# A fused two-layer block on one core: order of VectorE's compressed weights, TensorE's last modulation columns, and the first two half tiles of a mixer

## The chip, the cores and the metric

The kernel runs as one program on one core of a Trainium2 chip. The metric is the device time of one execution in microseconds. The kernel before took 1382.02 us, the median of three runs (1380.93 to 1382.14). All numbers of the profile come from one execution of their own, which took 1381.31 us.

## The reference, cut to what matters

Two different transformer blocks are run one after the other on x of 512 tokens and 1024 features, in float32.

```
x -> first block:  h = rms_norm(x); proj = h @ w_in
       attention over compressed, selected and window keys, each with a gate:
         kc, vc = compress(k_cmp), compress(v_cmp)          # 31 compressed positions
         p_c = softmax(q . kc - slope * distance) * valid   # "compressed weights"
         o = g0 * (p_c @ vc) + g1 * o_selected + g2 * o_window
       a causal convolution branch, a gated merge, w_out, residual
       conv FFN: w_up (1024 x 5632), 3 taps, silu(a) * v, w_down (2816 x 1024), residual
       final rms_norm
  -> second block: mod = silu(c) @ ada_w + ada_b             # 6 x 1024 "modulation"
       h = rms_norm(x) * (1 + scale) + shift
       proj = h @ w_in_2                                     # first tiles: the f logits
       sliding window attention, HGRN recurrence, w_out_2, gate, residual
       conv FFN with modulation, final rms_norm
```

With 8 blocks of 64 keys and a choice of 16, all blocks are selected, so the selected branch is causal attention over all keys, and so is the window branch.

## The kernel before, in words

Each weight matrix is cut into tiles of 128 output columns, numbered s through the whole program (`S_MERGE`, `S_DOWN`, `S_FH` and so on are first numbers of stages). A tile holds up to eight k of 128 rows. Every product is split for precision: ScalarE copies a raw tile to `w_hi` (L855), GpSimd subtracts to get `w_lo` (L788, function `lo`), and TensorE does three matmuls per k, `split_product` (L2135 to L2137): `w_hi` with `h_hi`, `w_hi` with `h_lo`, `w_lo` with `h_hi`. Each engine runs its own list in order; they meet at semaphores. ScalarE writes `w_hi` four tiles ahead, and `lo` follows it.

**Attention items.** The 32 items of the first block are (pair of heads, tile of queries, branch). In item j TensorE does the scores of j into banks 4 and 5 (two groups; it must wait until VectorE's row minimum of item j - 1 has read that bank), then half a merge tile (four k), then turns the weights of item j - 1 (L2408), which needs their scaling by VectorE, and in every second item multiplies two items with the values (L2379). The first four items have branch 0; from item 4 on, turns of the compressed weights `cp` (L2402) come in, and they need the semaphore `cp_ready` at 2. ScalarE does the exponentials (L1022), a copy (L1060) and in odd items a `w_hi`. VectorE's loop (from L1645) has in item j: `row_minimum(j)` (L1540), in items 1 to 4 one part of `compressed_weights` (two groups, each with a first part L1624 to L1630 and a second part L1620), convolution taps (L1527, from item 4), the copy of the turned weights of j - 1 (L1670) and `scaled_weights(j)` (L1636, L1640).

**Down projection of the first block.** 24 down parts of seven or eight k each; the modulation of the second block is computed beside them. SyncE loads 128 columns of `ada_w_2`, VectorE multiplies and adds them over eight k (`ada_reduce`, L1746 to L1756, into `ada_sum`), TensorE sums over partitions (`ada_tile`, L2440, one column of bank 6). The order of both is written out: TensorE takes column `m` after part n by the loop at L2522, VectorE by the same kind of loop. When all 48 are done VectorE forms shift and gain (L1850 to L1854).

**Into the next mixer.** The last down parts and the first four tiles of the second block (`S_FH`) are done in halves of 256 tokens, so that norm and matmul overlap. VectorE and ScalarE make 16 pieces of h (8 k for each half of the tokens): L1376, L900, L1386. TensorE's half tiles of half 0 wait for one piece per k. `column_sums(1)` (L2511) sums the squares of the second half and waits for `sums_added` (L1833, L1834); mean, root and inverse follow, then the turned inverses (L2519), then the pieces of half 1. For half 1, `second_halves` already takes the first two tiles in turn: k 0 to 3 of one, k 0 to 3 of the other, then k 4 to 7 alternating.

Of the kernel before, what the change touches and what calls it, by code (L numbers as in the profile page):

```python
# [18 lines left out]
KD = D // P  # L19
QT = T // P  # L20
# [23 lines left out]
S_FH, S_QH, S_KV2, S_PAIRED, S_GH = 126, 130, 134, 136, 144  # L44
# [114 lines left out]
def build(nc, a, out):  # L159
# [5 lines left out]
    with ctx:  # L165
# [24 lines left out]
        h_hi = sb("h_hi", [P, KD, T], F32R)  # L190
        msk_f = sb("msk_f", [P, DH], at=offset[0])
        yT = sb("yT", [P, KD, T], at=offset[0])
        h_lo = sb("h_lo", [P, KD, T], F32R)
# [1156 lines left out]
        def _(dve):  # L1350
# [261 lines left out]
            def compressed_weights(g, part):  # L1612

                x = cp[:, g * 16:(g + 1) * 16, 0:NCMP]
                low = stat[:, 32 + 16 * g:48 + 16 * g]
                if part:
                    for t in range(QT):
                        xt = cp[:, g * 16 + t * 4:g * 16 + t * 4 + 4, 0:NCMP]
                        v = cvalid[:, t, 0:NCMP].unsqueeze(1).to_broadcast([P, 4, NCMP])
                        ins = dve.tensor_tensor(xt, xt, v, ALU.mult)  # L1620
                    ins.then_inc(cp_ready, 1)
                    return
                dve.wait_ge(cexp_done, g + 1)
                link(dve.tensor_reduce(low, x, AX.X, ALU.add))  # L1624
                link(dve.reciprocal(low, low))
                dve.wait_ge(sig_ready, 1)
                gc = gates[:, :, 12 * g:12 * g + 12].rearrange("p t (i c) -> p t i c", c=3)[:, :, :, 0]
                by_tile = low.rearrange("p (t i) -> p t i", t=QT)
                link(dve.tensor_tensor(by_tile, by_tile, gc, ALU.mult))
                link(dve.tensor_tensor(x, x, low.unsqueeze(2).to_broadcast([P, 16, NCMP]), ALU.mult))  # L1630

            def scaled_weights(j):
                i, t, b = ITEMS1[j]
                q = 2 * (j % 2)
                dve.wait_ge(exp_done, 2 * j + 2)
                link(dve.reciprocal(stat[:, 8 + q:10 + q], stat[:, 4 + q:6 + q]))  # L1636
                for g in range(2):
                    x = sc[:, j % 2, g, 0:(t + 1) * P]
                    n = 12 * g + 3 * i + 1 + b
                    ins = dve.tensor_scalar(x, x, stat[:, 8 + q + g:9 + q + g], gates[:, t, n:n + 1], ALU.mult, ALU.mult)  # L1640
                ins.then_inc(p_ready, 1)
# [3 lines left out]
            for j in range(1, NI + 1):  # L1645
                if j < NI:
                    row_minimum(j)
                if j < 5:
                    compressed_weights((j - 1) // 2, (j - 1) % 2)
                if 4 <= j and IN_PSUM[1] + j - 4 < CONV_W:  # L1650
                    taps(1, IN_PSUM[1] + j - 4, IN_PSUM[1] + j - 3)
                c = j - LN_ADD + 1
                if 1 <= c < CC:
                    dve.wait_ge(tap_done, CC * CONV_W)
                    if c > 1:
                        dve.wait_ge(acc_added, c - 1)
                    dve.tensor_tensor(rstd[:, :], acc[:, 0, :] if c == 1 else rstd[:, :], acc[:, c, :],
                                      ALU.add).then_inc(acc_added, 1)
                c = j - LN_SQUARE - 1
                if 1 <= c < CC:  # L1660
                    dve.wait_ge(ln_sq, c + 1)
                    if c > 1:
                        dve.wait_ge(acc_added, CC + c - 2)
                    dve.tensor_tensor(z[:, 0, 0:T], z[:, 0, 0:T], z[:, c, 0:T], ALU.add).then_inc(acc_added, 1)
                m = j - 1
                L2 = (ITEMS1[m][1] + 1) * P
                dve.wait_ge(pw_turned, m + 1)
                if m >= 2:
                    dve.wait_ge(pv_done, m - 1)
                dve.tensor_copy(pT[:, m % 2, 1, 0:L2], ps[7][:, 0:L2]).then_inc(pw_copied, 1)  # L1670
                if j < NI:
                    scaled_weights(j)
                if j in LN_MEAN:
                    half = LN_MEAN.index(j)
                    cols = slice(half * 256, half * 256 + 256)
                    dve.wait_ge(ln_sum, half + 1)
                    for c in range(CC):
                        dve.scalar_tensor_tensor(out=acc[:, c, cols], in0=ps[3][:, cols], scalar=-1.0 / CONV_CH,
                                                 in1=acc[:, c, cols], op0=ALU.mult, op1=ALU.add).then_inc(ln_centred, 1)
                if j == LN_SUM:  # L1680
                    dve.wait_ge(ln_sqsum, 1)
                    dve.tensor_copy(stat[:, LN_SUMS], ps[3][:, 0:QT]).then_inc(ln_centred, 1)
# [449 lines left out]
        def _(pe):  # L2132
# [39 lines left out]
                elif s < s0 + KD and b != 1:  # L2172
                    ins.then_inc(half_done, 1)

            def second_halves(s, x, xl, ready):

                cols = COLS[1]
                for k, n in [(k, 0) for k in range(4)] + [(k, 1) for k in range(4)] + [(k, n) for k in range(4, KD) for n in range(2)]:
                    if n == 0:
                        ready(k)  # L2180
                    ins = split_product(ps[BANK[s + n]][:, cols], w_hi[(s + n) % 4][:, k, :], w_lo[(s + n) % 4][:, k, :],
                                        x[:, k, cols], xl[:, k, cols], k == 0, k == KD - 1)
                    if k == KD - 1:
                        ins.then_inc(tile_done, 1)

            def first_sum(b):
# [263 lines left out]
            def ffn_pe(s0, b):  # L2450
                for half in range(2):
                    for j in range(4):
                        if (half, j) == (1, 0):
                            second_halves(s0, h_hi, h_lo, lambda k: pe.wait_ge(half_lo, PIECES * b + KD + k + 1))
                        if half and j < 2:
                            continue
                        half_tile(b, s0 + j, half, h_hi, h_lo,
                                  ready=(lambda k: pe.wait_ge(half_lo, PIECES * b + KD * half + k + 1)) if j == 0 else None)
                        if (half, j) == (0, 1):
                            second_sum(b)  # L2460
                        if (half, j) == (1, 3) and b == 0:
                            ada_tile(ADA_EARLY - 1, (ADA_EARLY - 1) % 2, ADA_EARLY)
                with pe.Fori(0, FT // 2 - 1) as i:
                    for j in range(4):
                        s = s0 + 4 + j
                        pe.wait_ge(lo_done, i * 4 + (s + 1))
                        pe.wait_ge(freed["dve"], i * 4 + (FREED[s][1] - 4))
                        for k in range(KD):
                            ins = split_product(ps[BANK[s]][:, :], w_hi[s % 4][:, k, :], w_lo[s % 4][:, k, :],
                                                h_hi[:, k, :], h_lo[:, k, :], k == 0, k == KD - 1)  # L2470
                        ins.then_inc(tile_done, 1)
                        if b == 0 and j % 2:
                            n = ADA_EARLY + j // 2
                            ada_tile(i * 2 + n, n % 2, i * 2 + (n + 1))
# [47 lines left out]
            next_ada = itertools.count(ADA_EARLY + ADA_UP - 2)  # L2522
            for n in range(20):
                down_part(S_DOWN, n, parts(g_lo_done, 2) if n in (0, 2, 4) else None)
                if n < 18:
                    for _ in range(2 if n and n % 4 == 0 else 1):
                        m = next(next_ada)
                        ada_tile(m, m % 2, m + 1)
            for n in range(20, 24):
# [3 lines left out]
                if n == 20:  # L2533
                    column_sums(0)
            for half in range(2):
                for j in range(4):
                    if (half, j) == (1, 0):
                        second_halves(S_FH, h_hi, h_lo, lambda k: pe.wait_ge(half_lo, PIECES + KD + k + 1))
                    if half and j < 2:
                        continue  # L2540
                    half_tile(1, S_FH + j, half, h_hi, h_lo,
                              ready=(lambda k: pe.wait_ge(half_lo, PIECES + KD * half + k + 1)) if j == 0 else None,
                              between=(lambda: turn_inverse(1, 7, 2, range(2, QT))) if (half, j) == (0, 2) else None)
                    if (half, j) == (0, 1):
                        column_sums(1)
                    if (half, j) == (0, 3):
                        turn_inverse(1, 6, 0, range(QT))
            for s in range(S_QH, S_KV2):
                tile(s, h_hi, h_lo)

# [229 lines left out]
```

## Time and profile before

| what | before |
|---|---|
| median of the runs | 1382.02 us |
| profiled execution | 1381.31 us |
| its span | 1379.3 us |
| TensorE matmuls busy | 1367.5 us (99%) |
| VectorE busy | 770.4 us (56%) |
| ScalarE busy | 599.2 us (43%) |
| GpSimd busy | 600.4 us (44%) |
| granted TensorE clock | 9 tenths or more in all 40 slices |

The span runs from the first to the last instruction; the rest of the execution's time lies around it. Busy time of TensorE counts modelled ends of pipelined matmuls, so neighbouring ones overlap. In a timeline, a row is one instruction or several of a kind in sequence, with start, duration, engine and line; in brackets stands the idle time of the engine before it and what ended it. L numbers are lines of the kernel before.

### The profile page before, as it was taken

How to read it: one execution, taken by the hardware profiler on the slowest of the kernel's cores; microseconds unless marked ns; L12 is line 12 of the kernel's file. 1: busy time of each engine (PE TensorE's matmuls, PEld its weight loads, DVE VectorE, ACT ScalarE, POOL GpSimd, SP SyncE). 2: the span in 40 equal slices, each digit the busy share in tenths (PEclk: the TensorE clock that was granted, in tenths of full speed). 3: DMA queues.
4: the chain of work that ended last, by engine and by line, in shares of the span. 5: the costliest groups of instructions: out<-in, count | busy, mean ns of one | idle time of the engine just before them, and what ended most of it. 6: DMA issues, size and time to landing. Idle time of an engine off the chain costs nothing.

```text
span 1379.3 us, 20888 instructions
## 1 busy us (share of the span) xinstructions
PE 1367.5 (99%) x7650; PEld 1142.9 (83%) x7650; DVE 770.4 (56%) x1524; ACT 599.2 (43%) x1030; POOL 600.4 (44%) x322
## 2 busy tenths in 40 slices
PE   8999999999999999999999999999999999999998
PEld 7877777778998888888889978878998888888887
DVE  5897965456677566666873868633563223231222
ACT  6223555464254445443222524575364434442222
POOL 7532222226254444444543479623354444444441
PEclk9999999999999999999999999999999999999999
DMA  6931011015525444445662141021223332222221
GB/s 214 228 93 62 31 62 46 25 38 168 168 94 166 139 147 150 146 129 170 196 203 92 62 122 62 32 62 31 92 78 106 106 107 91 91 87 96 99 84 62
DMA packets 188309, 146.15 MB, mean 106 GB/s; under 512 B 21561, under 2 KB 186659, under 8 KB 188240
## 3 DMA queue, kind: packets, MB, share of 16 engines
q1 hardware_dynamic: 186528, 144.59, 34.0%
q8 instruction: 47, 0.77, 0.2%
q10 hardware_dynamic: 1200, 0.36, 0.1%
q0 software_dynamic: 512, 0.25, 0.1%
q14 instruction: 22, 0.18, 0.0%
HBM read 143.08 MB, written 2.10 MB: 105 GB/s over the span
## 4 chain that ended last, share of the span: by engine, by line
PE 91%; DVE 5%; DMA 3%; issue 1%; ACT 0%; DVEq 0%; ACTq 0%
PE ps L2135 27%; PE ps L2137 26%; PE ps L2136 26%; DMA ada<-in_ada_w 3%; DVE ps L1751 2%; PE ps L2584 2%; PE ps L2324 2%; PE ps L2379 1%; PE ps L2408 1%; PE ps L2655 1%; PE ps L2611 1%; PE ps L2640 1%; PE ps L2677 0%; PE ps L2218 0%; PE ps L2570 0%
## 5 line engine op out<-in xcount | busy, mean ns | idle before, releaser
L788 POOL TENSOR_TENSOR w_lo<-raw,w_hi 128x1024 fp32r<-128x1024 f32 (+2 forms) x224 | 515.4, 2304 | 709.0 <-ACT w_hi L855 439.4
L2135 PE MATMUL ps<-h_hi,w_hi 128*128 128x512 f32 (+1 forms) x1336 | 504.0, 377 | 0.6 <-DVE h_lo L1386 0.6
L2136 PE MATMUL ps<-h_lo,w_hi 128*128 128x512 f32 (+1 forms) x1336 | 493.4, 369 | 0.0
L2137 PE MATMUL ps<-h_hi,w_lo 128*128 128x512 f32 (+1 forms) x1336 | 493.2, 369 | 0.0
L2135 PEld LDWEIGHTS ps<-h_hi,w_hi 128*128 128x128 f32 x1336 | 251.7, 188 | 60.8 <-issue 17.6
L2137 PEld LDWEIGHTS ps<-h_hi,w_lo 128*128 128x128 f32 x1336 | 251.8, 188 | 43.1
L2136 PEld LDWEIGHTS ps<-h_lo,w_hi 128*128 128x128 f32 x1336 | 251.9, 189 | 40.1 <-issue 0.5
L855 ACT ACTIVATE w_hi<-raw 128x1024 fp32r<-128x1024 f32 (+2 forms) x136 | 133.7, 985 | 254.5 <-PE ps L2137 245.1
L1125 ACT ACTIVATE w_hi<-raw 128x1024 fp32r<-128x1024 f32 x88 | 93.2, 1059 | 217.9 <-PE ps L2137 217.9
L2135 PE MATMUL ps<-g_hi,w_hi 128*128 128x512 f32 (+1 forms) x394 | 146.6, 372 | 0.0
L2136 PE MATMUL ps<-g_lo,w_hi 128*128 128x512 f32 (+1 forms) x394 | 144.6, 367 | 0.0
L2137 PE MATMUL ps<-g_hi,w_lo 128*128 128x512 f32 (+1 forms) x394 | 144.4, 367 | 0.0
L1751 DVE SCALAR_TENSOR_TENSOR ps<-ada,cond,ps 128x128 f32<-128x128 f32 x288 | 102.5, 356 | 10.3
L2137 PEld LDWEIGHTS ps<-g_hi,w_lo 128*128 128x128 f32 x394 | 74.3, 188 | 12.2
L2135 PEld LDWEIGHTS ps<-g_hi,w_hi 128*128 128x128 f32 x394 | 74.3, 189 | 11.7
L2136 PEld LDWEIGHTS ps<-g_lo,w_hi 128*128 128x128 f32 x394 | 74.4, 189 | 11.5
L1790 DVE SCALAR_TENSOR_TENSOR sq<-ps,small,sq 128x511 f32<-128x511 f32 x44 | 33.0, 750 | 88.4 <-ACT sq L1132 85.4
L2060 DVE SCALAR_TENSOR_TENSOR xT<-ps,small,xT 128x256 f32<-128x256 f32 (+1 forms) x22 | 13.3, 604 | 106.1 <-PE ps L2137 106.1
L1527 DVE SCALAR_TENSOR_TENSOR ps<-z,small,ps 128x512 f32<-128x512 f32 x106 | 70.4, 747 | 0.0
L1784 DVE TENSOR_TENSOR hn<-ps,sq 128x512 f32<-128x512 f32 x22 | 15.2, 691 | 85.9 <-ACT sq L1136 85.9
L1022 ACT ACTIVATE sc<-sc,stat 128x128 f32<-128x128 f32 (+3 forms) x64 | 35.5, 555 | 35.0 <-DVE stat L1540 34.9
L1670 DVE COPY pT<-ps 128x128 f32<-128x128 f32 (+3 forms) x32 | 15.7, 490 | 54.3 <-PE ps L2379 32.1
(362 smaller groups left out, 1700.8 us busy)
## 6 DMA issues: line engine op xcount, KB each, us to landing
ada<-in_ada_w SPq DMA_DIRECT2D x48, 512.0 KB, 3.8
raw<-in_ffn_w_up SPq DMA_DIRECT2D x22, 1024.0 KB, 4.9
raw<-in_w_up SPq DMA_DIRECT2D x22, 1024.0 KB, 4.9
raw<-in_w_in SPq DMA_DIRECT2D x21, 1024.0 KB, 5.0
raw<-in_ffn_w_down SPq DMA_DIRECT2D x8, 896.0 KB, 6.2
raw<-in_w_down SPq DMA_DIRECT2D x8, 896.0 KB, 4.7
raw<-in_w_in SPq DMA_DIRECT2D x16, 256.0 KB, 3.8
raw<-in_w_out SPq DMA_DIRECT2D x4, 1024.0 KB, 5.2
```

What stands on the lines that cost most here:

```text
L788: pool.tensor_tensor(w_lo[slot % 4][:, 0:nk, :], part[:, :, slot % 2 * P:(slot % 2 + 1) * P], w_hi[slot % 4][:, 0:nk, :].bitcast(F32), ALU ...
L855: act.activation(w_hi[s % 4][:, 0:nk, :], part[:, :, s % 2 * P:(s % 2 + 1) * P], ACT.Copy).then_inc(hi_done, 1)
L1022: act.activation(x, x, ACT.Exp, scale=-1.0, bias=stat[:, 2 * (j % 2) + g:2 * (j % 2) + g + 1], accum_out=stat[:, 4 + 2 * (j % 2) + g:5 + 2 ...
L1125: act.activation(w_hi[s % 4][:, :, :], part[:, :, s % 2 * P:(s % 2 + 1) * P], ACT.Copy).then_inc(hi_done, 1)
L1527: ins = dve.scalar_tensor_tensor(out=out, in0=src, scalar=w, in1=was, op0=ALU.mult, op1=ALU.add)
L1751: dve.scalar_tensor_tensor(out=acc, in0=src, scalar=c, in1=acc, op0=ALU.mult, op1=ALU.add).then_inc(ada_scaled, 1)
L1790: dve.scalar_tensor_tensor(out=u[:, t, 1:T], in0=src[:, 0:T - 1], scalar=col(wname, m + wide), in1=u[:, t, 1:T], op0=ALU.mult, op1=ALU.add ...
L2135: pe.matmul(out_ap, w, x, start=first, stop=False, **kw)
L2136: pe.matmul(out_ap, w, xl, start=False, stop=False, **kw)
L2137: return pe.matmul(out_ap, wl, x, start=False, stop=last, **kw)
L2324: pe.matmul(ps[4 + g][:, 0:L], qT[grp, i, t * P:(t + 1) * P], kT[grp, b, 0:L], start=True, stop=True).then_inc(qk_done, 1)
L2584: ins = pe.matmul(bank[:, at:at + nq], keys[:, hd, t * P:(t + 1) * P], qd[n % 2][:, hd, q0:q0 + nq], start=True, stop=True)
```

## The change

Three orders are changed; no instruction is added or removed.

1. VectorE, items 1 to 4: the part of `compressed_weights` moves from behind the row minimum of item j to behind the scaling of item j.
2. TensorE, down parts: columns are taken two at a time after parts 4, 8 and 12 only, and one after parts 16, 17 and 18 each, in place of two after 16 and one after 17.
3. TensorE, first half of the tokens in the next mixer: tiles `S_FH` and `S_FH + 1` are taken in turn (`second_halves` becomes `two_halves`, used for both halves).

```diff
-                if j < 5:
-                    compressed_weights((j - 1) // 2, (j - 1) % 2)
                 if 4 <= j and IN_PSUM[1] + j - 4 < CONV_W:
                     taps(1, IN_PSUM[1] + j - 4, IN_PSUM[1] + j - 3)
...
                 if j < NI:
                     scaled_weights(j)
+                if j < 5:
+                    compressed_weights((j - 1) // 2, (j - 1) % 2)
...
-            def second_halves(s, x, xl, ready):
-
-                cols = COLS[1]
+            def two_halves(s, half, x, xl, ready):
+
+                cols = COLS[half]
                 for k, n in [(k, 0) for k in range(4)] + [(k, 1) for k in range(4)] + [(k, n) for k in range(4, KD) for n in range(2)]:
                     if n == 0:
                         ready(k)
+                    if half == 0 and k == 0:
+                        pe.wait_ge(lo_done, s + n + 1)
+                        wait_bank(pe, s + n)
                     ins = split_product(ps[BANK[s + n]][:, cols], w_hi[(s + n) % 4][:, k, :], w_lo[(s + n) % 4][:, k, :],
                                         x[:, k, cols], xl[:, k, cols], k == 0, k == KD - 1)
-                    if k == KD - 1:
+                    if k == KD - 1 and half:
                         ins.then_inc(tile_done, 1)
...
-                if n < 18:
-                    for _ in range(2 if n and n % 4 == 0 else 1):
+                if n < 19:
+                    for _ in range(2 if n in (4, 8, 12) else 1):
                         m = next(next_ada)
                         ada_tile(m, m % 2, m + 1)
...
             for half in range(2):
-                for j in range(4):
-                    if (half, j) == (1, 0):
-                        second_halves(S_FH, h_hi, h_lo, lambda k: pe.wait_ge(half_lo, PIECES + KD + k + 1))
-                    if half and j < 2:
-                        continue
+                two_halves(S_FH, half, h_hi, h_lo, lambda k: pe.wait_ge(half_lo, PIECES + KD * half + k + 1))
+                if half == 0:
+                    column_sums(1)
+                for j in range(2, 4):
                     half_tile(1, S_FH + j, half, h_hi, h_lo,
-                              ready=(lambda k: pe.wait_ge(half_lo, PIECES + KD * half + k + 1)) if j == 0 else None,
                               between=(lambda: turn_inverse(1, 7, 2, range(2, QT))) if (half, j) == (0, 2) else None)
-                    if (half, j) == (0, 1):
-                        column_sums(1)
-                    if (half, j) == (0, 3):
-                        turn_inverse(1, 6, 0, range(QT))
+                if half == 0:
+                    turn_inverse(1, 6, 0, range(QT))
```

The call in the up projections' `ffn_pe` becomes `two_halves(s0, 1, ...)` with the same order as before.

## Rows read from the trace of the kernel before

**Rows 1.** Page: busy us (share of span) x instructions.
```profile
PE 1367.5 (99%) x7650; PEld 1142.9 (83%) x7650; DVE 770.4 (56%) x1524; ACT 599.2 (43%) x1030; POOL 600.4 (44%) x322
```

**Rows 2.** Waits of TensorE: waited for: us in total, times, longest.
```profile
PE ps L2440 <- DVE ada_sum L1756: 1.0, 1, 1.0
```

**Rows 3.** Timeline of TensorE, items 3 to 5: start us, us, what [idle].
```profile
141.55 1.13 PE L2324 MATMUL ps<-kT,qT 64*128 64x512 f32 x4
...
147.06 0.49 PE L2324 MATMUL ps<-kT,qT 64*128 64x128 f32 x4
...
150.11 0.39 PE L2137 MATMUL ps<-h_hi,w_lo 128*128 128x512 f32 x1
151.44 1.09 PE L2408 MATMUL ps<-ident,sc 128*128 128x128 f32 x8 [0.94 <-DVE sc L1640]
152.46 0.70 PE L2324 MATMUL ps<-kT,qT 64*128 64x256 f32 x4
...
155.97 0.38 PE L2402 MATMUL ps<-ident,cp 128*31 128x128 f32 x2
```

**Rows 4.** Timeline of VectorE, items 2 and 3.
```profile
139.82 0.55 DVE L1540 CUSTOM_DVE_ANT_0 sc<-ps,sq 128x384 f32<-128x384 f32 x1
...
140.77 2.47 DVE L1620 TENSOR_TENSOR cp<-cp,cvalid 128x124 f32<-128x124 f32 x4
...
145.69 0.66 DVE L1624 TENSOR_REDUCE stat<-cp 128x16 f32<-128x496 f32 x1
...
146.68 0.18 DVE L1629 TENSOR_TENSOR stat<-stat,gates 128x16 f32<-128x16 f32 x1
146.89 0.67 DVE L1630 TENSOR_TENSOR cp<-cp,stat 128x496 f32<-128x496 f32 x1
...
148.26 3.12 DVE L1640 TENSOR_SCALAR sc<-sc,stat,gates 128x512 f32<-128x512 f32 x2
```

**Rows 5.** Timeline of GpSimd, the same stretch.
```profile
140.12 2.38 POOL L788 TENSOR_TENSOR w_lo<-raw,w_hi 128x1024 fp32r<-128x1024 f32 x1 [7.67 <-ACT w_hi L855]
148.26 2.39 POOL L788 TENSOR_TENSOR w_lo<-raw,w_hi 128x1024 fp32r<-128x1024 f32 x1 [5.75 <-ACT w_hi L855]
```

**Rows 6.** Timeline of ScalarE: ends of the exponentials of items 2 and 3.
```profile
141.53 0.19 ACT L1022 ACTIVATION_READ_ACCUMULATOR sc<-sc,stat 128x1 f32 x1
...
146.53 0.19 ACT L1022 ACTIVATION_READ_ACCUMULATOR sc<-sc,stat 128x1 f32 x1
```

**Rows 7.** Timeline of TensorE, modulation columns behind down parts 15 and 16.
```profile
718.30 0.28 PE L2440 MATMUL ps<-ones,ada_sum 128*128 128x1 f32 x2
718.44 0.48 PE L2135 MATMUL ps<-g_hi,w_hi 128*128 128x512 f32 x1
...
723.31 0.28 PE L2440 MATMUL ps<-ones,ada_sum 128*128 128x1 f32 x2
...
724.79 0.49 PE L2135 MATMUL ps<-g_hi,w_hi 128*128 128x512 f32 x1
```

**Rows 8.** Timeline of TensorE, first two half tiles of the next mixer.
```profile
762.06 0.28 PE L2135 MATMUL ps<-h_hi,w_hi 128*128 128x256 f32 x1
...
762.42 0.28 PE L2135 MATMUL ps<-h_hi,w_hi 128*128 128x256 f32 x1
...
765.50 0.39 PE L2135 MATMUL ps<-h_hi,w_hi 128*128 128x256 f32 x1 [0.29 <-DVE h_lo L1386]
...
769.46 0.50 PE L2511 MATMUL ps<-ones,rstd 128*128 128x1 f32 x4
```

**Rows 9.** Timeline of VectorE, last piece and last square sum.
```profile
765.60 0.48 DVE L1386 SCALAR_TENSOR_TENSOR h_lo<-ps,small,h_hi 128x256 fp32r<-128x256 f32 x1 [0.15 <-ACT h_hi L900]
...
767.59 0.48 DVE L1834 SCALAR_TENSOR_TENSOR sq<-hn,stat,sq 128x256 f32<-128x256 f32 x1
```

**Rows 10.** Timeline of GpSimd, `w_lo` of the second and fourth tile.
```profile
758.42 2.41 POOL L788 TENSOR_TENSOR w_lo<-raw,w_hi 128x1024 fp32r<-128x1024 f32 x1 [1.21 <-ACT w_hi L855]
...
767.90 2.42 POOL L788 TENSOR_TENSOR w_lo<-raw,w_hi 128x1024 fp32r<-128x1024 f32 x1 [4.21 <-ACT w_hi L855]
```

More of the change, by code:

```diff
@@ L2453, in ffn_pe @@
                         if (half, j) == (1, 0):
-                            second_halves(s0, h_hi, h_lo, lambda k: pe.wait_ge(half_lo, PIECES * b + KD + k + 1))
+                            two_halves(s0, 1, h_hi, h_lo, lambda k: pe.wait_ge(half_lo, PIECES * b + KD + k + 1))
                         if half and j < 2:
```

## The prediction

> **What bounds the kernel now.** I read the page's busy shares first: TensorE (PE) is busy for 1367.5 us of a span of 1379.3 us [rows 1]. So nothing is won by making another engine faster; only places where TensorE stands still can move the end. The second view is the list of who waited for whom, cut to TensorE. The change touches three entries of it: 1.0 us for `ada_sum` [rows 2], 0.9 us for `sc`, which the timeline prints as idle time [rows 3], and short waits for `h_lo`, one of which stands in [rows 8]. The third view is the timeline around each of them, one engine at a time, because a wait that is removed has to be followed to whatever is late next. TensorE's modelled ends hide part of a wait (the idle time printed is measured from a modelled end), so I measure a wait as actual start minus the start that the regular spacing would give. The reader should check in the timelines that matmuls of 512 columns start every 0.23 us and those of 256 columns every 0.12 us (0.36 us for the three products of one k) [rows 3, 8].
>
> **Edit 1: compressed weights behind the scaling (items 1 to 4).** VectorE's order in item j was: row minimum of j, compressed weights, copy of the turned weights, scaling of j. The wait it is about: the turns of item 3 start at 151.44, where the last product before them started at 150.11, so they were due at 150.34 and are 1.10 us late; they wait for the scaling of item 3, which took 3.12 us for two products [rows 3, 4]. That scaling is long not because of work put before it but because GpSimd's `w_lo` ran from 148.26 to 150.65 [rows 5]. The same is seen at 140.77, where four products of `cp` and `cvalid` took 2.47 us while GpSimd's `w_lo` lasted from 140.12 to 142.50 [rows 4, 5]. So an instruction of VectorE with two inputs in SBUF that starts inside a `w_lo` finishes only after it. The reductions and the row minimum (one input in PSUM) are not held: the row minimum at 139.82 has its usual 0.55 us [rows 4].
>
> Now the new order. In item 1 the scaling ends at about 139.82, where the row minimum of item 2 used to start [rows 4]. The compressed weights of group 0 stand there now. By their rows in item 3, the first small product (`stat`, `gates`) starts 0.99 us after the reduction and the large one ends 1.87 us after it [rows 4]. So the small product would start at 140.81, inside the `w_lo` that ScalarE's work, which the edit does not touch, starts at 140.12 [rows 5]. It is held to 142.54, and the large one then needs 0.67 us: 143.25. Only then comes the row minimum of item 2; its first group needs 0.55 us and is done at 143.83. TensorE needs exactly this before the scores of item 3 may overwrite their bank, and these scores were issued at 141.55 [rows 3]. They go at 143.89: **+2.34 us**. Queued behind them in TensorE's order is a quarter of the merge tiles, the turns and the value products, all of which shift.
>
> From there: the exponentials of item 2 end 1.35 us after its first row minimum (141.72 [rows 6] against 140.37), so they end at 145.2; the scaling of 2, the second part of the weights (unheld some 0.8 us: 2.47 us less the 1.73 us up to 142.50) and the row minimum of 3 follow and end at 148.3; TensorE reaches the scores of item 4 at 147.06 + 2.34 = 149.40 [rows 3] and does not wait. The exponentials of 3 end at 149.24 (146.72 before [rows 6]), the scaling of 3 at 150.6. GpSimd's `w_lo` follows them by way of ScalarE's copy and `w_hi`, so it slips by the same 2.52 us to 150.78: it misses the scaling. TensorE wants it at 150.34 + 2.34 = 152.68, so the old wait goes: **-1.10 us**. What is late next: compressed weights of group 1 start at 150.47, their small product at 151.46 falls into the slipped `w_lo` (to 153.17), they end at 153.92, the row minimum of item 4 at 154.23; the scores of item 5 would be due at 152.46 + 1.24 = 153.70 [rows 3] and go at 154.29: **+0.59 us**. Last, the second part for group 1 now ends after taps, copy and scaling of item 4, at 157.93, against 155.97 + 1.83 = 157.80 for the turns that read it [rows 3]: **+0.13 us**. Sum for edit 1: **+1.96 us**. I find no later wait that absorbs it, since TensorE has none in the rest of this stage [rows 2].
>
> Bounds. If nothing of the compressed weights were held by `w_lo`, the weights would end at 139.82 + 1.87 = 141.69, the row minimum of 2 would be ready at 142.29 and the scores late by 0.80 us, the 1.10 us would go, and no other wait would form: -0.30 us. If the slipped `w_lo` also caught the scaling of item 3 (it would have to start before 150.06, not at 150.78), the weights of group 1 would end 0.6 us later: +2.6 us. I take +1.96, nearest to the rows, which show the hold with every start known.
>
> One operation has no held example in these rows: the small product of 16 elements. If only the large one were held, all would be 0.2 us earlier.
> The Trainium skill, page "SBUF — State Buffer", section "Who interferes with whom", says that a VectorE instruction with two SBUF inputs contends with a GpSimd instruction that reads SBUF, that whoever starts first keeps the pair of ports for its whole length, and it names no least size. By that rule the small product is held too (the 2.34 us as above; 2.1 us without it). It is the rule that speaks against this edit, and rows 4 and 5 agree with it in the two long groups.
>
> **Edit 2: last modulation columns.** After down part 16 TensorE did two columns (45 and 46), after part 17 one (47). The first started at 723.31; an unhindered column costs 0.14 us on TensorE (718.30 to 718.44); the tile behind the second started at 724.79. So 724.79 - 723.31 - 0.27 = **-1.21 us** goes when column 46 is taken after part 17 [rows 7]. VectorE finished column 46 just before 724.6, and part 17 now ends near 728.5. Column 47 met no wait at its old place behind part 17 (it is no entry of [rows 2]) and is now taken a whole part later. So no wait replaces this one. VectorE then folds the 48 columns into the modulation, which the first half pieces need only at 756. Bounds: 1.0 us (the printed idle [rows 2]) to 1.21 us.
>
> **Edit 3: first two half tiles of the next mixer in turn.** Before, TensorE went through eight k of the first half tile alone, from 762.06, at the pace at which VectorE and ScalarE deliver pieces of h, then through the second half tile, and reached the column sums at 769.46 [rows 8]. Unhindered, 16 k of 0.36 us end at 762.06 + 5.76 = 767.82: 1.64 us of waiting. In the new order k 0 to 3 of both tiles come first, so piece 4 is wanted at 764.94, 5 at 765.66, 6 at 766.38 and 7 at 767.10; the last piece is done at 766.08 [rows 9]. None is late. The second tile's `w_lo` is done at 760.83 [rows 10], before 763.50, when TensorE turns to that tile. But the column sums behind them need VectorE's last square added, which ends at 767.59 + 0.48 = 768.07 whatever TensorE does [rows 9]. TensorE goes on at 768.12: **-1.34 us**, and 0.3 us turn into a new wait. From the sums on, every step (means, root, inverse, pieces of the second half) is started by TensorE and moves with it. Bounds: -1.64 us to the rival below. Instructions are only reordered: none is added in edit 1, 2 or 3.
>
> **Sum.** +1.96 - 1.21 - 1.34 = -0.59 us. The profiled execution took 1381.31 us (span 1379.3 us and 2.0 us around it), so it would become 1380.7 us. It lies 0.7 us under the median 1382.02 of the runs shown; from the median the forecast is **1381.4 us**, which is no change: 0.2% (2.8 us) is about what can be told apart.
>
> **Rivals.**
> A. The hold does not strike the compressed weights, and edit 1 is a small gain: -0.30 - 1.21 - 1.34 = -2.85, so 1379.2 us. For it: the small product was never seen held. Against it: the four `cvalid` products right beside it were.
> B. Slower: a `w_lo` catches the last square sum. Today the product at 767.59 starts 0.3 us before GpSimd's `w_lo` at 767.90 (2.42 us) [rows 9, 10]. If that order turned, the sum would end at 770.6 instead of 768.07, TensorE would reach the column sums 1.1 us later than before instead of 1.34 earlier: +1.96 - 1.21 + 1.1 = +1.9, 1383.9 us. It decides as soon as `w_lo` starts before 767.59. Against it: both hang on the same square of ScalarE, and neither is moved by TensorE.
> C. The turn-taking gains nothing, since the wait for pieces merely moves to the column sums: +1.96 - 1.21 = +0.75, 1382.8 us. Against it: the square sum is ready 1.4 us before TensorE used to come.
> D. Edit 1 does what its order suggests, the wait of 1.10 us goes and no row minimum is late: -1.10 - 1.21 - 1.34 = -3.65, 1378.4 us. Against it: the compressed weights stand between two row minima in either order, and 1.9 us of them now delay the one that TensorE needs first.
>
> **How the numbers follow.** Forecast 0.68, A 0.10, D 0.05, B 0.08, C 0.09. Faster by over 0.2% needs A or D: 0.13, with A on the line. Slower by over 0.2% (past 1384.8) needs B with edit 1 at its upper bound: 0.05. Within: 0.82. The range runs from near A to B: 1378.9 to 1384.0.
>
> **What would show it.** Right: a TensorE wait of about 2.3 us before scores of item 3, released by VectorE's row minimum; `stat` or `cp` products of the compressed weights about 1.8 us long beside `w_lo`; no wait before the turns of item 3; no wait over 0.2 us at the last modulation columns; no `h_lo` wait in the first half tiles and a wait of about 0.3 us at the column sums. Wrong: the scores of item 3 start near 141.6 or 142.3, or the column sums near or after the 769.5 of before (less what came earlier).

## The result, and the profile after

| | before | after |
|---|---|---|
| median of 12 runs each, same chips | 1380.95 us (1379.62 to 1384.11) | 1383.58 us (1383.39 to 1385.32) |
| profiled execution, span | 1381.31, 1379.3 us | 1383.87, 1381.8 us |
| TensorE busy | 1367.5 us | 1370.3 us |
| mean granted clock of TensorE in it | 1.000 | 0.997 |

The ratio is 1.0018 [1.0009, 1.0026]: slower by 2.5 us, where no change (-0.6 us) was forecast. A repeat (below) gave 1.0017 [1.0008, 1.0026]. No instruction was added, yet TensorE, which is nearly always busy, is busy for 2.8 us more. So part of the loss is slower work and not standing still.

The busy line of the profile's page after, then TensorE's waits (waited for: total, times, longest):

```profile
PE 1370.3 (99%) x7650; PEld 1144.8 (83%) x7650; DVE 772.1 (56%) x1524; ACT 598.9 (43%) x1030; POOL 601.7 (44%) x322
```
```profile
PE ps L2327 <- DVE stat L1540: 2.7, 2, 2.3
```

The waits for `ada_sum` [rows 2] and `h_lo` of the half tiles [rows 8] are gone, and one for the row minimum is there, twice. TensorE's timeline around both (L2327 is L2324 of before, L2411 is L2408; answers to [rows 3]):

```profile
140.49 0.60 PE L2411 MATMUL ps<-ident,sc 128*128 128x128 f32 x4
143.34 2.08 PE L2327 MATMUL ps<-kT,qT 64*128 64x512 f32 x4 [2.25 <-DVE stat L1540]
145.36 0.79 PE L2135 MATMUL ps<-h_hi,w_hi 128*128 128x512 f32 x1
145.95 0.63 PE L2136 MATMUL ps<-h_lo,w_hi 128*128 128x512 f32 x1
146.38 0.63 PE L2137 MATMUL ps<-h_hi,w_lo 128*128 128x512 f32 x1
...
147.93 0.39 PE L2135 MATMUL ps<-h_hi,w_hi 128*128 128x512 f32 x1
...
153.90 0.39 PE L2137 MATMUL ps<-h_hi,w_lo 128*128 128x512 f32 x1
154.13 1.04 PE L2411 MATMUL ps<-ident,sc 128*128 128x128 f32 x8
155.66 0.91 PE L2327 MATMUL ps<-kT,qT 64*128 64x256 f32 x4 [0.49 <-DVE stat L1540]
```

Two things are to be seen. The turns of item 3 now follow their neighbour by 0.23 us: their old wait is gone. And the products of 512 columns start 0.43 us apart from 145.95 to 147.66, then 0.23 us again. The granted clock shows it too (a row is window: its length, then busy us and instructions of PE, PEld, DVE, ACT and POOL, then PEclk, the DMA share and GB/s):

```profile
143.00:148.00 5.00, 4.66 (x11) 2.70 (x12) 4.15 (x16) 2.89 (x9) 0.00 (x0) 0.66 0.00 0
148.00:153.00 5.00, 5.00 (x37) 3.95 (x36) 2.33 (x6) 2.12 (x4) 0.96 (x1) 1.00 0.01 3
```

The records put TensorE at half clock (1.2 GHz) from 144.33 to 147.74, and at the full 2.4 GHz on both sides. The execution of before has no such stretch between its first 10 us and its last two.

VectorE, and GpSimd beside it, show where the wait comes from (answers to [rows 4, 5]):

```profile
139.28 0.66 DVE L1624 TENSOR_REDUCE stat<-cp 128x16 f32<-128x496 f32 x1
139.98 0.25 DVE L1625 RECIPROCAL stat<-stat 128x16 f32<-128x16 f32 x1
140.26 1.72 DVE L1629 TENSOR_TENSOR stat<-stat,gates 128x16 f32<-128x16 f32 x1
142.01 0.67 DVE L1630 TENSOR_TENSOR cp<-cp,stat 128x496 f32<-128x496 f32 x1
142.72 0.56 DVE L1540 CUSTOM_DVE_ANT_0 sc<-ps,sq 128x384 f32<-128x384 f32 x1
...
143.21 0.55 DVE L1540 CUSTOM_DVE_ANT_0 sc<-ps,sq 128x384 f32<-128x384 f32 x1
...
152.18 0.66 DVE L1624 TENSOR_REDUCE stat<-cp 128x16 f32<-128x496 f32 x1
...
153.16 1.39 DVE L1629 TENSOR_TENSOR stat<-stat,gates 128x16 f32<-128x16 f32 x1
```
```profile
139.58 2.36 POOL L788 TENSOR_TENSOR w_lo<-raw,w_hi 128x1024 fp32r<-128x1024 f32 x1 [7.66 <-ACT w_hi L855]
152.04 2.48 POOL L788 TENSOR_TENSOR w_lo<-raw,w_hi 128x1024 fp32r<-128x1024 f32 x1 [10.10 <-ACT w_hi L855]
```

The product of 16 elements, 0.18 us long when free [rows 4], takes 1.72 and 1.39 us and ends with the `w_lo` beside it. The reduction at 152.18 starts inside the same `w_lo` and takes the 0.66 us that it takes elsewhere. The row minimum that the prediction gives for this, at 139.82, began before the `w_lo` of 140.12 and could not tell; one that begins inside a `w_lo`, at 155.35 in e7 below, takes 0.42 us, as its like at 155.49 in the kernel before, which had none beside it.

The other two edits. TensorE at the modulation columns behind parts 15 and 16 (answers to [rows 7]), then at the end of the first two half tiles ([rows 8]):

```profile
721.66 0.28 PE L2443 MATMUL ps<-ones,ada_sum 128*128 128x1 f32 x2
721.80 0.48 PE L2135 MATMUL ps<-g_hi,w_hi 128*128 128x512 f32 x1
...
726.67 0.28 PE L2443 MATMUL ps<-ones,ada_sum 128*128 128x1 f32 x2
726.80 0.48 PE L2135 MATMUL ps<-g_hi,w_hi 128*128 128x512 f32 x1
...
764.28 0.28 PE L2135 MATMUL ps<-h_hi,w_hi 128*128 128x256 f32 x1
...
769.92 0.28 PE L2137 MATMUL ps<-h_hi,w_lo 128*128 128x256 f32 x1
770.34 0.61 PE L2514 MATMUL ps<-ones,rstd 128*128 128x1 f32 x4
```

A column costs 0.13 us. From 764.28 the 48 products run without a gap; the sums are due at 764.28 + 5.76 = 770.04 and start 0.30 us late. Both as forecast. But later there is a second stretch at half clock, 953.29 to 956.70, right behind three groups of eight one-column sums (L2617; the first and the third are `head_sum`):

```profile
950.46 0.95 PE L2617 MATMUL ps<-ones,qd 128*128 128x1 f32 x8
951.27 1.03 PE L2617 MATMUL ps<-ones,hn 128*128 128x1 f32 x8
952.16 1.03 PE L2617 MATMUL ps<-ones,qd 128*128 128x1 f32 x8
953.05 0.58 PE L2135 MATMUL ps<-h_hi,w_hi 128*128 128x512 f32 x1
953.44 0.63 PE L2136 MATMUL ps<-h_lo,w_hi 128*128 128x512 f32 x1
...
956.79 0.39 PE L2135 MATMUL ps<-h_hi,w_hi 128*128 128x512 f32 x1
```

**Where the 2.5 us of span are.** I matched the matmuls of both executions by their number in order (both have 7650) and took the difference of their starts. It moves here:

| place | moves by us | forecast |
|---|---|---|
| first 20 us (loads; not the change) | -0.53 | |
| scores of item 3, first group | +2.32 | +2.34 |
| scores of item 3, second group | +0.47 | not seen |
| half clock behind them | +1.53 | not seen |
| turns of item 3 | -1.10 | -1.10 |
| scores of item 5 | +0.71 | +0.59 |
| `cp_ready` | +0.02 | +0.13 |
| edit 2 | -1.13 | -1.21 |
| edit 3 | -1.25 | -1.34 |
| half clock near 953 | +1.55 | not seen |
| elsewhere, in steps of at most 0.1 | -0.1 | |
| sum | +2.5 | |

### The profile page after: what moved, and what is told of

It is laid out like the page before. It is cut to its first block, busy times and chain, and to the rows that moved or that the text cites. A ratio compares the mean times of both kernels' runs of the same rounds, so it can differ in the third digit from the quotient of the medians.

```text
span 1381.8 us, 20887 instructions
## 1 busy us (share of the span) xinstructions
PE 1370.3 (99%) x7650; PEld 1144.8 (83%) x7650; DVE 772.1 (56%) x1524; ACT 598.9 (43%) x1030; POOL 601.7 (44%) x322
## 4 chain that ended last, share of the span: by engine, by line
PE 97%; DVE 2%; DMA 0%; ACT 0%; issue 0%; SPq 0%; DVEq 0%; ACTq 0%
PE ps L2135 29%; PE ps L2136 28%; PE ps L2137 28%; PE ps L2583 2%; PE ps L2327 2%; PE ps L2382 1%; PE ps L2411 1%; PE ps L2654 1%; PE ps L2610 1%; PE ps L2639 1%; DMA x_in<-in_x 0%; PE ps L2676 0%; PE ps L2443 0%; PE ps L2569 0%; PE ps L2617 0%; PE ps L2295 0%
## 5 line engine op out<-in xcount | busy, mean ns | idle before, releaser
L1784 DVE TENSOR_TENSOR hn<-ps,sq 128x512 f32<-128x512 f32 x22 | 15.2, 691 | 85.9 <-ACT sq L1136 85.9
```

## The experiments

Each ratio is to the kernel before on the same chip, with its 95% interval (it is not exactly the quotient of the two medians). Each kernel was run 11 times, e1 8, e9 12 and e13 6 times, and each profile is one execution.

| run | median us | before us | ratio |
|---|---|---|---|
| e1_weights_only | 1385.26 | 1381.36 | 1.0025 [1.0015, 1.0036] |
| e2_columns_and_turns | 1378.58 | 1381.36 | 0.9983 [0.9974, 0.9992] |
| e3_warm_wait | 1383.39 | 1381.36 | 1.0012 [1.0003, 1.0021] |
| e5_no_hold | 1383.29 | 1381.36 | 1.0010 [1.0001, 1.0019] |
| e6_free_scaling | 1378.57 | 1381.89 | 0.9976 [0.9968, 0.9985] |
| e7_no_hold_late | 1380.18 | 1381.89 | 0.9990 [0.9981, 0.9998] |
| e8_columns_only | 1380.83 | 1381.89 | 0.9992 [0.9983, 1.0001] |
| e9_turns_only | 1380.76 | 1381.89 | 0.9991 [0.9983, 1.0000] |
| e10_changed_again | 1383.53 | 1381.53 | 1.0017 [1.0008, 1.0026] |
| e11_split_sums | 1382.56 | 1381.53 | 1.0005 [0.9996, 1.0014] |
| e12_split_and_warm | 1382.42 | 1381.53 | 1.0006 [0.9997, 1.0015] |
| e13_free_and_split (6 runs) | 1377.30 | 1381.53 | 0.9970 [0.9958, 0.9982] |
| e14_warm_fit | 1381.87 | 1381.87 | 1.0001 [0.9992, 1.0010] |
| e15_split_warm_fit | 1380.60 | 1381.87 | 0.9994 [0.9985, 1.0003] |
| e16_split_again | 1382.41 | 1381.87 | 1.0007 [0.9998, 1.0016] |

**The parts alone.** e1 has only edit 1, e2 only edits 2 and 3, e8 only edit 2, e9 only edit 3 (each hunk of the change as it stands, the others undone).

> Edit 1 alone. Theory 1 (waits of about 2.0 us in the items, and TensorE's clock at 1.2 GHz for 3.4 us right after its 2.3 us wait, about 1.9 us more): about 3.9 us slower than before, a wait of 2.3 us at the scores of item 3, a stretch of half clock starting there. Theory 2 (the half clock of the changed kernel is chance and not tied to the wait): about 2.0 us slower, half clock there in some executions only. Rival (edit 1 is harmless, the loss is from edits 2 and 3): within 0.5 us of before.

> Edits 2 and 3 without edit 1. If the terms of the prediction hold: -1.2 - 1.3 = 2.5 us faster than before. If the half clock near 953 us of the changed kernel comes with edits 2 and 3 (TensorE reaches the three groups of column sums at another time), only 0.9 us faster with such a stretch in the profile; if it comes with edit 1's shift, no such stretch.

> Edit 2 alone: 1.2 us below before, no wait at the last modulation columns. If the half clock near 950 us, seen in all four kernels with edits 2 and 3 and in neither without, comes with edit 2: it is in this profile and only 0.5 us or nothing is left of the gain. If it is chance, it is in this profile or not without tie to the edit.

> Edit 3 alone: 1.3 us below before, a wait of 0.15 to 0.3 us at the column sums in place of the waits for h_lo. As in e8 the profile also shows whether the half clock near 950 us comes with this edit.

Edit 1 alone costs 3.9 us by the medians (2.1 to 5.0 by the interval), twice the 1.96 of the forecast; edits 2 and 3 together win 2.8 us and singly 1.1 each, near the 2.55, 1.21 and 1.34 of theirs (the intervals of e8 and e9 reach 1; their traces show the moves of -1.13 and -1.25). So the miss lies in edit 1 alone. In e1's profile the same wait is followed by half clock for 6.83 us, and the shift from the second group's start to the end of it grows by 3.0 us, not 1.5. This profiled execution is the slowest of e1's eight. Compared at one mean granted clock, e1 is 2.1 us (0.998: 1384.35 against 1382.23) and 2.2 us (0.999: a single run, 1382.80, against 1380.62) above before, near the moves of the table without the half clock (3.95 - 1.53 = 2.42). TensorE's timeline and clock there:

```profile
144.69 2.55 PE L2324 MATMUL ps<-kT,qT 64*128 64x512 f32 x4 [2.25 <-DVE stat L1540]
147.17 0.79 PE L2135 MATMUL ps<-h_hi,w_hi 128*128 128x512 f32 x1
```
```profile
145.00:150.00 5.00, 5.00 (x11) 2.80 (x11) 3.50 (x14) 3.21 (x10) 0.00 (x0) 0.50 0.00 0
```

**Is the wait GpSimd's hold?** e5 and e7 keep edit 1 and put the two `w_lo` off. `scores_ready` counts VectorE's row minima, so in e5 they start behind the row minimum of item 2 and behind the first one of item 4:

```diff
+                if s in (S_MERGE + 4, S_MERGE + 5):       # e5
+                    pool.wait_ge(scores_ready, 6 if s == S_MERGE + 4 else 9)
                 lo(s)
```

e7 has `cp_ready`, 2 (the end of the compressed weights) as the second wait in place of `scores_ready`, 9.

> The changed kernel with GpSimd's w_lo of two merge tiles started only after the row minimum of item 2 and of item 4, so that no w_lo runs beside the compressed weights. If the hold by w_lo is what makes VectorE late: the small stat product takes 0.18 us instead of 1.72, the scores of item 3 wait 0.8 us instead of 2.3, no half clock there, the scores of item 5 do not wait; edit 1 then gains about 0.3 us and the whole is 2 to 3 us faster than before. If the hold is not the cause (the compressed weights are late by themselves): scores of item 3 still 2 us late, time as the changed kernel.

> The changed kernel as in e5_no_hold, but the w_lo of S_MERGE + 5 waits for the end of the compressed weights (cp_ready), since in e5 it fell on two taps (3.54 us) and made TensorE wait 1.87 us. Theory (all of edit 1's loss is the hold and the half clock that follows the long wait): scores of item 3 wait 0.8 us, no other wait in the items, no half clock near 145 us, time 2 to 3 us below before. Rival (the order itself loses): the same time as e5 or more than before.

In e5, VectorE's small product is free and TensorE's wait is short, but the second `w_lo` now falls on two convolution taps, and TensorE waits for the `cp` behind them (VectorE, GpSimd and TensorE of e5):

```profile
140.93 0.18 DVE L1631 TENSOR_TENSOR stat<-stat,gates 128x16 f32<-128x16 f32 x1
...
152.40 3.54 DVE L1529 SCALAR_TENSOR_TENSOR acc<-z,small,acc 128x512 f32<-128x512 f32 x2
```
```profile
152.35 2.37 POOL L788 TENSOR_TENSOR w_lo<-raw,w_hi 128x1024 fp32r<-128x1024 f32 x1 [7.00 <-DVE stat L1542]
```
```profile
142.47 1.60 PE L2329 MATMUL ps<-kT,qT 64*128 64x512 f32 x4 [0.72 <-DVE stat L1542]
...
158.18 0.38 PE L2407 MATMUL ps<-ident,cp 128*31 128x128 f32 x2 [1.87 <-DVE cp L1622]
```

So e5's time says little of the hold (the hold moved); e7's does: only the 0.72 us wait is left, no half clock stands near 145, and it is 1.7 us faster than before (2 to 3 were expected) where the changed kernel is 2.0 to 2.6 us slower. The scores of item 3 are 0.79 us late in both, the forecast's 0.80 for "nothing held", and the second group again 0.47 more. With the old wait gone, edit 1's items then cost +0.09 us up to 157 in e7, not the -0.30 of rival A. Another 0.45 us come at 161.5 to 162.5, because the hold has moved here too (VectorE, then GpSimd of e7):

```profile
155.69 3.06 DVE L1529 SCALAR_TENSOR_TENSOR acc<-z,small,acc 128x512 f32<-128x512 f32 x2
...
159.06 2.42 DVE L1642 TENSOR_SCALAR sc<-sc,stat,gates 128x256 f32<-128x256 f32 x2
```
```profile
155.17 2.37 POOL L788 TENSOR_TENSOR w_lo<-raw,w_hi 128x1024 fp32r<-128x1024 f32 x1 [10.64 <-DVE cp L1622]
158.12 2.88 POOL L788 TENSOR_TENSOR w_lo<-raw,w_hi 128x1024 fp32r<-128x1024 f32 x1 [0.58 <-ACT w_hi L857]
```

Two taps take 3.06 us for 1.41, the scaling behind them 2.42 for 0.73, and TensorE's turns and scores come late by it. So the hold is shown as the cause of the long wait at item 3, and no run here frees the items of it altogether. What is left at item 3 without it (0.79 + 0.47 us) already eats the 1.10 us that edit 1 wins.

e6 asks what the aim of edit 1 was worth: old VectorE order, edits 2 and 3, and only the `w_lo` that held the scaling of item 3 put off until the scaling of item 4 is done (`p_ready` counts scalings).

```diff
+                if s == S_MERGE + 5:
+                    pool.wait_ge(p_ready, 5)
                 lo(s)
```

> Edits 2 and 3, VectorE's order in the items as before, and instead of edit 1 GpSimd's w_lo of tile S_MERGE + 5 waits until the scaling of item 4 is done. If the wait of 1.1 us in the kernel before was made by that w_lo and not by the compressed weights: the scaling of item 3 takes 1.0 us instead of 3.12, TensorE does not wait for it, no row minimum is late, and the time is -1.1 - 1.2 - 1.3 = 3.6 us below before and 1.1 us below e2. If the order of VectorE made it: the wait stays and the time is that of e2.

The scaling takes 1.00 us in place of 3.12 [rows 4] and the turns wait no more (VectorE, TensorE of e6):

```profile
147.58 1.00 DVE L1642 TENSOR_SCALAR sc<-sc,stat,gates 128x512 f32<-128x512 f32 x2
```
```profile
149.44 0.39 PE L2139 MATMUL ps<-h_hi,w_lo 128*128 128x512 f32 x1
149.67 1.04 PE L2413 MATMUL ps<-ident,sc 128*128 128x128 f32 x8
```

It is 3.3 us faster than before, against 2.8 for e2. These two stand on different chips and their intervals overlap, so the times alone do not tell them apart. The trace does: the 1.10 us at the turns are gone and nothing is late behind them, though the `w_lo`, now at 152.51, holds two taps (3.07 us), for which TensorE does not wait. Moving the holder does what moving the held work could not.

**Is the lowered clock the rest?** e3 lets TensorE work through its wait with filling products; these write into a free bank and add no result. e14 does the same with half as many.

```diff
             for j in range(1, NI + 2):
+                if j == 3:
+                    keep_warm(3, 20)      # e3; e14: keep_warm(3, 10)
                 if j < NI:
                     scores(j)
```

> The changed kernel with 20 extra products of 128 columns into a free bank before the scores of item 3, which fill TensorE's wait of 2.3 us and add no work behind it. Theory 1: the wait's length stays but the clock does not fall, so 1.7 to 2.0 us faster than the changed kernel, about 0.6 to 1 us slower than before. Theory 2: the same time as the changed kernel.

> The changed kernel with 10 filling products (20 matmuls of 0.11 us, 2.2 us in all) in TensorE's order before the scores of item 3. They write into the bank that the item before no longer needs and add no result. Theory (the idle wait costs twice: 2.3 us itself, and 1.7 to 2 us by a half-clock stretch behind it): the scores of item 3 start where they did, near 143.3, no half-clock stretch near 145, and the time is 1.7 to 2 us below the changed kernel: 1381.6 to 1382. Rival 1 (the half clock costs nothing net, or comes from something else): 1383.4 as the changed kernel. Rival 2 (filling costs what it saves, as the 4.4 us of filling did): the scores start at 144 or later and the time is again 1383.4.

e3 gained nothing that the intervals can tell, and by my fault: one filling product is two matmuls of 0.11 us, so 20 last 4.4 us and overrun a wait of 2.3 (TensorE of e3):

```profile
140.84 4.63 PE L2221 MATMUL ps<-ident,ones 128*128 128x128 f32 x40
145.40 1.13 PE L2327 MATMUL ps<-kT,qT 64*128 64x512 f32 x4
```

The clock stays full, but the scores are 2.1 us later than in the changed kernel: one loss in place of another. e14 fits the wait (TensorE, then its clock):

```profile
140.83 2.40 PE L2221 MATMUL ps<-ident,ones 128*128 128x128 f32 x20
143.26 1.60 PE L2327 MATMUL ps<-kT,qT 64*128 64x512 f32 x4
144.79 0.50 PE L2135 MATMUL ps<-h_hi,w_hi 128*128 128x512 f32 x1
```
```profile
145.00:150.00 5.00, 5.00 (x36) 3.93 (x36) 3.66 (x13) 2.92 (x7) 0.00 (x0) 1.00 0.02 3
```

The scores start where they did (143.26 against 143.34), and the time falls from 1.0018 and 1.0017 to 1.0001 of before: 2.2 us, though this compares across chips.

**The second stretch.** e10 is the changed kernel again; e11 and e16 move the first of the three groups of one-column sums two k earlier, so that products of 512 columns stand between; e12 and e15 add e3's and e14's filling.

```diff
-            tile(S_GH + 2, h_hi, h_lo, part=(0, 4))
+            tile(S_GH + 2, h_hi, h_lo, part=(0, 2))
             head_sum(2)
+            tile(S_GH + 2, h_hi, h_lo, part=(2, 4))
```

> The changed kernel itself, on the chip of the next three, so that they can be compared with it. Expected 2.0 to 3.5 us over before, hardly an execution under 1383 us.

> The changed kernel with the three groups of one-column sums near 950 us (24 products, 2.6 us of TensorE with one column each) parted: the first group two k of the tile earlier. Theory (the half clock of 3.4 us found near 950 us in six of ten profiles follows this row of one-column products): no such stretch in the profile, and 1 to 1.7 us faster than the changed kernel in the median. Rival (it is chance and tied to nothing there): same median, a stretch there in the profile in about half the cases.

> e11_split_sums with the 20 filling products of e3_warm_wait in TensorE's wait of 2.3 us. Theory (each half-clock stretch costs 1.7 us, one follows the long wait): 1.7 to 2.0 us faster than e11 and about as before or 0.5 us faster, with no half clock until the tail. Rival (the wait alone costs what edit 1 costs, 4 us): same as e11.

> The changed kernel with the first of the head sums moved two k forward (so that the one-column products do not all follow each other) and the 10 filling products before the scores of item 3. Theory: 1.7 to 2 us below e16, the same kernel without the filling, so near 1380.7, no half-clock stretch near 145 or 950. Rival: equal to e16 (1382.5).

> The changed kernel with the first of the head sums moved two k forward, run again beside e15. Both theories: 1382.5, a half-clock stretch near 145 and a wait of 2.3 us before the scores of item 3.

The pair that settles it ran on one chip: e15 takes 1380.60 us and e16, the same without filling, 1382.41. That is 1.8 us for 20 matmuls that compute nothing; nine of e15's eleven runs lie below e16's fastest, 1381.92. e12 (overlong filling, 0.1 us below e11) shows e3's fault again. Over all profiles: behind the wait of 2.25 us before the scores of item 3 the clock fell in 5 of 5 (after, e1, e10, e11, e16); behind e5's wait of 1.87 us at 158 in 0 of 1; behind 0.72 us in 0 of 2 (e5, e7); behind a filled wait in 0 of 4 (e3, e12, e14, e15). e1's run at 0.999 suggests that it need not fall in every execution. Near 950 it fell in 8 of 12 profiles with the three groups in a row and in 0 of 5 with the first one split off. On one chip the split gave 1.0 us (e11 against e10) and 1.3 us (e15 against e14), the first of them within the scatter of the runs. So the tie to the sums in a row is likely, on 17 executions, and why they should lower the clock is not shown. e1 and e2 have one more stretch, from 15.2 to 18.6 and from 15.3 to 18.7, near the loads at the start, where nothing was changed. The kernel before is one of the four of the 12 without it, but its other runs were not all like the profiled one: in the set beside e14, those with a mean granted clock of 0.999 or 1.000 have a median of 1380.5 us (12 runs), those with 0.998 have 1382.1 (11), those with 0.997 have 1383.9 (4). So most of the spread goes with the mean clock, in such steps; where in those runs it fell no trace shows.

**The best version.** e13 is e6 with the split.

> e6_free_scaling with the parted sums. If the stretch near 950 us goes by this, 0.5 to 0.9 us faster than e6 in the median (half of its executions had one), near 1377.3 us, and the fastest of all; if not, as e6.

1377.30 us, 0.9970 [0.9958, 0.9982]: no wait of TensorE in the items, no half clock between start and tail, and a spread of 1.3 us in six runs, where before had 4.0 in 28. On other chips e6, without the split, had 0.9976, so the split's own share is not told apart by these intervals.

## Why the prediction was wrong

**What held.** The hold of the small product by `w_lo` and its place, and the scores of item 3 late by 2.32 us for 2.34. The Trainium skill, page "SBUF — State Buffer", section "Who interferes with whom", has no least size for that hold, and the trace agrees: 16 elements waited 1.5 us. The old wait's 1.10 us went, scores of item 5 were late by 0.71 (0.59), edit 2 gave 1.13 (1.21), edit 3 gave 1.25 (1.34) with the new 0.3 us wait at the column sums. Rivals A, C and D did not come: e7 had to be built to get A's condition at item 3, e9 shows edit 3's gain, and the late row minimum rules out D. B did not come either: the last square sum starts 0.30 us before `w_lo`, as before:

```profile
769.81 0.48 DVE L1834 SCALAR_TENSOR_TENSOR sq<-hn,stat,sq 128x256 f32<-128x256 f32 x1
```
```profile
770.11 2.41 POOL L788 TENSOR_TENSOR w_lo<-raw,w_hi 128x1024 fp32r<-128x1024 f32 x1 [4.21 <-ACT w_hi L855]
```

**What failed** is the term "+1.96 us" of edit 1, with its sentence "I find no later wait that absorbs it": nothing absorbed it, but something multiplied it. It measured +3.95 us, by two omissions.
1. "They go at 143.89: +2.34 us" treats the scores as one. They are two groups, and the second needs the second row minimum, which VectorE ends 0.47 us after the first. Before, both were long done. The same 0.47 us stands in e5 and e7 with another size of the first wait. It is the smaller of the two: it would have made the sum -0.1 us and left the forecast at "no change".
2. The wait has a price beyond its length: the granted clock falls to half behind it, which cost 1.53 us here and 3.0 us in e1. That made a loss beyond the interval out of a change near zero. It is shown by taking it away alone: 1.8 us between e15 and e16. The Trainium skill, page "TensorE: Matmul & The Clock Gate", section "Terms", prices such a stretch at its length times the share of clock pulses withheld. Half of 3.41 us makes an estimate of 1.7 us by the Trainium skill; the traces have 1.53 and 1.55 us, somewhat less.

With both corrected the sum is +3.95 - 1.13 - 1.25 = +1.6 us. The medians say +2.0 to +2.6 us. The rest I put down to how often and how long the clock falls in the two places; how the shares of before and after differ there was not measured with enough runs, and it stays open. At a full clock the change is worth +0.0 us (3.95 - 1.53 - 2.38 = +0.04), and e15's runs at 0.999 have a median of 1380.5 us, like those of before.

The range (1378.9 to 1384.0) held the time, but only because B's price had widened it; B's cause did not come, so that was luck. The 0.05 was for slower by over 0.2%, which did not happen (0.18%); but except for B (0.08) and C (0.09) no case had a loss at all, and none had a price for an idle TensorE above its length.

## What to carry to other kernels

Count a long wait of an otherwise full TensorE dearer than its length: 2.3 us cost 3.9 here (2.3 of the wait and 1.5 of slower products behind it), and filling it with products that compute nothing (just as long as the wait, no longer) gave 1.8 back. When GpSimd holds a VectorE instruction on the critical path, move the GpSimd instruction to where no held instruction is waited for, as in e6. In e5 and e7, and in the changed kernel, the hold only chose the next victim. Before one trusts a difference of one or two microseconds, the mean granted clock of each run should stand beside its time.

## What the runs showed of the hardware

- The granted clock fell in a kernel whose TensorE is 99% busy, behind 2.25 us of idle time (5 of 5 profiles) and at 24 one-column sums in a row (8 of 12; 0 of 5 with eight of them moved away), for 3.41 us or, in e1 and in e5 near 952, 6.83 us. It did not fall behind 1.87 us (e5) or 0.72 us (e5, e7). Each 3.41 us cost 1.5 to 1.6 us in the traces and stands as a step of about 1.7 us in the runs.
- During such a stretch products of 512 columns start 0.43 us apart instead of 0.23.
- A free scaling of two products takes 1.00 us, and one beside `w_lo` took 3.12: GpSimd's subtraction also holds VectorE's TENSOR_SCALAR, which has one tensor and its scalars in `stat` and `gates`, not only products of two tensors. It holds the convolution taps as well, 3.54 us for 1.41 (e5).
- It does not hold a reduction (0.66 us at 152.18 inside the `w_lo` of 152.04, after) or the row minimum, which reads PSUM (0.42 us at 155.35 inside the `w_lo` of 155.17, e7).
